# Chunk loop of a Mamba-2 mixer: the order of GpSimd's two additions, the place of ScalarE's scaling, and a second buffer for B and C

## The reference

```
def ssd_chunked(x, dt, a_neg, bm, cm):
    ...
    acs = jnp.cumsum((dt * a_neg)..., axis=2)
    seg = acs[:, :, :, None] - acs[:, :, None, :]
    decay_in = jnp.exp(jnp.where(tri, seg, NEG_INF))
    cb = jnp.einsum('bctgn,bcsgn->bctsg', cc, bc)
    y_diag = jnp.einsum('bctsg,bctsgh,bcsghp->bctghp', cb, decay_in, xdt)
    states = jnp.einsum('bcsgn,bcsgh,bcsghp->bcghpn', bc, decay_out, xdt)
    ... # prev: the state ahead of each chunk, from a scan over chunks
    y_off = jnp.einsum('bctgn,bcghpn,bctgh->bctghp', cc, prev, jnp.exp(acs))
    return y_diag + y_off

y = y_fwd + y_bwd + d_skip * xs
y = y * silu(z)            # then an RMS norm per group of 256 columns
```

## Time and profile before

| | us |
|---|---|
| median of 3 executions | 2486.51 |
| lowest and highest | 2482.69, 2488.45 |
| the profiled execution, its time | 2485.22 |
| the profiled execution, its span | 2483.40 |

### The profile page before, as it was taken

The page is one execution under the profiler, slowest core; times in us unless marked ns, Lnnn a source line. Parts: engine busy times, 40 slices in busy tenths (PEclk is TensorE's granted clock), DMA queues, the critical chain, the costliest instruction groups (busy, mean ns, idle before and its releaser), DMA issues.

```text
span 2483.4 us, 33046 instructions
## 1 busy us (share of the span) xinstructions
PE 2426.9 (98%) x12882; PEld 2072.2 (83%) x12882; DVE 1375.8 (55%) x1561; ACT 998.4 (40%) x1737; POOL 1263.1 (51%) x814
## 2 busy tenths in 40 slices
PE   7999999999999999999999999998999999999999
PEld 6989997887888888887898899977878888888887
DVE  4476557738655546428345765586385555544332
ACT  4345567613444344212024465585144344431110
POOL 3242113323977877666633311142349877866664
PEclk9999999999999999999999999999999999999999
DMA  4434444231222212654333334442212222226544
GB/s 160 136 114 125 134 139 149 81 119 68 85 79 91 85 68 85 217 178 132 130 121 94 110 128 151 134 136 90 89 64 102 85 70 100 83 90 201 174 141 142
DMA packets 102964, 290.68 MB, mean 117 GB/s; under 512 B 7800, under 2 KB 30328, under 8 KB 101112
## 3 DMA queue, kind: packets, MB, share of 16 engines
q1 hardware_dynamic: 80360, 255.73, 30.4%
q10 hardware_dynamic: 22456, 32.90, 4.1%
HBM read 229.84 MB, written 58.75 MB: 116 GB/s over the span
## 4 chain that ended last, share of the span: by engine, by line
PE 81%; DVE 9%; ACT 4%; POOL 3%; issue 2%; DMA 1%; SPq 0%; ACTq 0%; DVEq 0%; POOLq 0%
PE PS L690 20%; PE PS L694 20%; PE PS L693 20%; PE PS L775 3%; PE PS L779 3%; PE PS L778 3%; PE PS L945 2%; PE PS L934 2%; POOL WL L629 2%; DVE HL L1780 1%; PE PS L1116 1%; PE PS L1081 1%; PE PS L924 1%; PE PS L923 1%; ACT LG L1501 1%
## 5 line engine op out<-in xcount | busy, mean ns | idle before, releaser
L605 POOL CAST WH<-RAW 128x1024 fp32r<-128x1024 f32 x156 | 184.5, 1182 | 905.5 <-PE PS L690 327.1
L690 PE MATMUL PS<-HH,WH 128*128 128x512 f32 x1264 | 496.4, 393 | 3.6 <-ACT QS L1668 2.6
L694 PE MATMUL PS<-HH,WL 128*128 128x512 f32 x1264 | 493.3, 390 | 0.0
L693 PE MATMUL PS<-HL,WH 128*128 128x512 f32 x1104 | 430.5, 390 | 0.0
L607 POOL TENSOR_TENSOR WL<-RAW,WH 128x1024 fp32r<-128x1024 f32 x156 | 396.8, 2543 | 12.5
L690 PEld LDWEIGHTS PS<-HH,WH 128*128 128x128 f32 x1264 | 237.4, 188 | 56.5 <-DVE HL L1780 3.5
L694 PEld LDWEIGHTS PS<-HH,WL 128*128 128x128 f32 x1264 | 237.3, 188 | 51.9
L690 PE MATMUL PS<-AR,WH 128*128 128x512 f32 x704 | 276.0, 392 | 2.3 <-DVE X L2208 1.8
L694 PE MATMUL PS<-AR,WL 128*128 128x512 f32 x704 | 275.9, 392 | 0.0
L693 PE MATMUL PS<-AR,WH 128*128 128x512 f32 x704 | 275.2, 391 | 0.0
L775 PE MATMUL PS<-WH,HH 128*128 128x256 f32 (+1 forms) x896 | 261.0, 291 | 1.7 <-ACT KN L1307 1.3
(11 more groups left out here) (274 smaller groups left out, 4677.3 us busy)
## 6 DMA issues: line engine op xcount, KB each, us to landing
RAW<-wst SPq DMA_DIRECT2D x156, 512.0 KB, 3.5
TOE<-toe_d SPq DMA_DIRECT2D x64, 512.0 KB, 3.7
act_d<-CVV SPq DMA_DIRECT2D x22, 1024.0 KB, 4.0
ARL<-act_d SPq DMA_DIRECT2D x88, 256.0 KB, 3.3
RAW<-wst SPq DMA_DIRECT2D x20, 1024.0 KB, 4.9
RAWB<-wst SPq DMA_DIRECT2D x20, 1024.0 KB, 4.9
XBS<-xbc_d SPq DMA_DIRECT2D x24, 512.0 KB, 4.2
xbc_d<-CV ACTq DMA_DIRECT2D x16, 512.0 KB, 3.6
```

Of the source, the lines that this page charges most:

```text
L605: nc.gpsimd.tensor_copy(hi, raw).then_inc(hi_done, 1)
L690: ins = nc.tensor.matmul(out, wh, xh, start=first, stop=False, skip_group_check=onto)
L693: nc.tensor.matmul(out, wh, xl, start=False, stop=False, skip_group_check=onto)
L694: return nc.tensor.matmul(out, wl, xh, start=False, stop=last, skip_group_check=onto)
```

## The change

It has three parts.

1. POOL adds the forward part (`Y1`) to `Y3` first, and the backward part (`Y2`) after it. In `scan` the two blocks change places, and with them the waits for `y12_done` and `y2_ready`.
2. ACT scales the backward part into `Y2` between the first and the second pair of exponentials, after v, and no longer after the second pair.
3. `BC` becomes two buffers, one for even and one for odd chunks. ACT's copy into it waits for the masks and the state of two chunks ago, no longer for those of the chunk before. The new buffers lie in a stretch that is free during the chunk loop.

```diff
-        BC = work("BC", [P, 2, GROUPS, P])
+        BC = place("BC", [P, 2, 2, GROUPS, P], u_at + 25856)
...
                     step.then(nc.gpsimd.tensor_tensor(by_head(Y3[:]), xs, per_head(par_("d_skip")), ALU.mult))
+                    if c:
+                        pool.wait_ge(y12_done, 1 + l * LINKS + c)
+                        ins = nc.gpsimd.tensor_tensor(Y3[:], Y3[:], Y1[:], ALU.add)
+                        if c < LINKS:
+                            step.then(ins)
                     if c < LINKS:
                         pool.wait_ge(y2_ready, l * LINKS + c + 1)
                         ins = nc.gpsimd.tensor_tensor(Y3[:], Y3[:], Y2[:], ALU.add)
-                        if c:
-                            step.then(ins)
-                    if c:
-                        pool.wait_ge(y12_done, 1 + l * LINKS + c)
-                        ins = nc.gpsimd.tensor_tensor(Y3[:], Y3[:], Y1[:], ALU.add)
                     ins.then_inc(y3_ready, 1)
...
-                            last = nc.tensor.matmul(PS[:, 7, g * 256:(g + 1) * 256], BC[:, 0, g, :],
+                            last = nc.tensor.matmul(PS[:, 7, g * 256:(g + 1) * 256], BC[:, par, 0, g, :],
...
-                    act.wait_ge(w_masked, 2 + n * 2)
-                    if c:
-                        act.wait_ge(sf_full, l * LINKS + c)
-                    A(BC[:].rearrange("p a g n -> p (a g n)"), bank(1), ACT.Copy).then_inc(bst_ready, 1)
+                    if n:
+                        act.wait_ge(w_masked, n * 2)
+                    if c >= 2:
+                        act.wait_ge(sf_full, l * LINKS + c - 1)
+                    A(BC[:, par].rearrange("p a g n -> p (a g n)"), bank(1), ACT.Copy).then_inc(bst_ready, 1)
...
                         if j == 1:
                             v_scaled(c)
-                    if c < LINKS:
-                        act.wait_ge(yo_full, n + 1)
-                        act.wait_ge(chunk_done, 1 + n)
-                        for h in range(HEADS):
-                            cols = slice(h * HD, (h + 1) * HD)
-                            last = A(Y2[:, cols], PS[:, 6, cols], ACT.Copy, scale=EACS[:, c, 8 + h:9 + h])
-                        last.then_inc(y2_ready, 1)
+                        if j == 1 and c < LINKS:
+                                act.wait_ge(yo_full, n + 1)
+                                act.wait_ge(chunk_done, 1 + n)
+                                for h in range(HEADS):
+                                    cols = slice(h * HD, (h + 1) * HD)
+                                    last = A(Y2[:, cols], PS[:, 6, cols], ACT.Copy, scale=EACS[:, c, 8 + h:9 + h])
+                                last.then_inc(y2_ready, 1)
...
-                                TT(SEG[par][:, 2 * g], SEG[par][:, 2 * g], BC[:, 1, g, :].unsqueeze(1).to_broadcast((P, 4, P)),
+                                TT(SEG[par][:, 2 * g], SEG[par][:, 2 * g], BC[:, par, 1, g, :].unsqueeze(1).to_broadcast((P, 4, P)),
```

## The result

The changed kernel takes 2502.53 us (median of 6 executions, 2501.4 to 2504.99) against 2484.97 for the kernel before in the same comparison (6 executions, 2482.69 to 2488.45): ratio 1.0071, 95% interval 1.0058 to 1.0084. It is 17.6 us slower. The forecast was slower by 12, 2498, with a range to 2502: the sign and the mechanism came as forecast, the size did not, and the time lies 0.5 us above the range. In the two traces chunks 0 to 6 of the two loops hold 17.0 us of the difference; outside them the traces differ by +1.6 (ahead of the first loop), +1.4 (between the loops) and -1.7 us (behind), which is not explained here.

A forecast was written before the change was run, and what follows sets the result against it. PE was taken as nearly the bound, with a few stalls. Chunks 1 to 6 add 4.89 and 5.74 us, chunks 0 add 1.0: 11.6 us, profiled 2485.2 to 2496.8, median 1.3 higher, 2498 us; range 2489 to 2502.

The forecast's parts named there:

- What bounds a chunk: Chunk loops: PE nearly the bound, with stalls where DVE's mask L2144 is late; chunks of 8.35 and 9.25 us alternate.
- rule A: DVE operations with two SBUF inputs and POOL's exclude each other, first starter first; DVE ends 0.55 after POOL, POOL begins 0.54 after DVE's start.
- The collision that costs: POOL's L655 of the next chunk starts 0.18 before group 1's mask, delaying PE: 9.73 us a chunk, chunks 1 to 5.
- The second BC buffer at nothing: On ACT, it removes a 6.8 us wait in 7 places, but the new wait for `yo_full` swallows it: cost nothing.
- Chunk 0, +0.5 a layer: First chunk of each layer: masks end later, by +0.1 to +1.1 us; 0.5 taken in each layer.
- The sum: Both chunk loops: 4.89 and 5.74 for chunks 1 to 6, plus 1.0 for chunks 0, makes 11.6 us slower.
- Behind the loop PE runs on without DVE or POOL in between: After the chunk loop: the loss is carried to the end whole.
- The wording of the lock in the Trainium skill: DVE holds the lock for its whole instruction: +0.35 a chunk more, some 3.5 us over 10 chunks, 2501.5 us.
- R1: Half the collision: L655 starts after group 1's mask has begun; every chunk 9.01 us, 2491 us in all; chance 0.12.
- R3: Faster: POOL's second add falls into DVE's free time, nothing stalls; chunks 8.35 us, 2481.4 us in all; chance 0.10.
- R2: Slower still: POOL's second add gets ahead of group 0's first mask; 10.1 us a chunk, 2502 us; chance 0.08.
- R4: No change: the gain of the early `y3_ready` and the new collision offset each other, within 5 us; chance 0.04.

The follow-up runs named there:

- experiment 4: The changed kernel with only L655 on POOL waiting for both masks of the chunk before; 2487.55 us, ratio 1.0011 to the kernel before.
- experiment 5: The changed kernel with L655 waiting for the previous chunk's masks and POOL's add of Y2 for its own chunk's masks; 2480.08 us, ratio 0.9978 to before.
- experiment 3: Kernel before with only the second BC buffer and its later waits, 2485.15 us; changed kernel without that part, 2500.28 us.
- The second trace: The changed kernel run once more, unaltered, in a single execution for another trace; 2502.12 us, no ratio.
- experiment 8: The kernel of experiment 5, with the last chunk's add of Y1 on POOL also waiting for both masks; 2478.32 us, ratio 0.9970 to before.
- experiment 6: The changed kernel with PE repeating group 0 products in its stall, chunks 0 to 5: 8 products 2503.42 us, 4 products 2494.97 us.
- experiment 1: The kernel before with only POOL's order changed, Y1 added first and Y2 after it; 2480.62 us, ratio 0.9981 to before.

## Why the prediction was right and where it was wrong

- *What bounds a chunk, and rule A.* Right. The offsets of chunk 2 above stand within 0.07 us of the forecast ones (only PE's idle time there is 0.89, where about 1.1 was forecast), and experiments 4 and 5 take the two collisions away one after the other with the chunk lengths that the rule gives, 9.00 and 8.35.
- *"The collision that costs", 9.73 us a chunk.* Right, 9.73 in most of the chunks; and chunk 6 at 9.01 was 9.00.
- *The second BC buffer at nothing.* Right (experiment 3).
- *Chunk 0, +0.5 a layer, bounds +0.1 and +1.1.* Slightly low. At full clock it is 9.25 to 9.28 against 8.66 and 8.56, +0.6 and +0.7. L655 comes between the masks there as well: with L655 held back (experiment 4) chunk 0 is 8.55.
- *The sum.* This is the step that failed. "Chunks 1 to 5: 5 x 9.73 = 48.65" takes every chunk at full clock; that longer stalls could change PE's clock was put at nothing, without a reason, in the sum and in every rival. The runs show 5.1 us there. Of the 17.0 us by which the two loops grew (70.29+68.62 against 61.43+60.47), 11.6 were forecast; slow chunks hold 1.20+0.16+1.53+1.68=4.6 beyond 9.73, chunk 0 of the first layer 0.5, in a stretch at half clock as well, and chunk 0's own under-sizing the last 0.3. The second trace repeats the total, and filling the stall takes 4.9 out of it (67.00+67.02, 12.1 more than before, where 11.6 were forecast). So the forecast was in effect one for a kernel whose clock holds. The whole time of that filled kernel is 8.8 us above before (7 to 14 by the interval), so the times bear the 12.1 out only roughly.
- *"Behind the loop PE runs on without DVE or POOL in between".* Not so: PE waits for ACT and DVE there too (experiment 8). For the loss in chunks 0 to 6, which delays all engines, it made no visible difference.
- *Why the clock falls* is shown in so far as PE's stalls bring it about: filling them keeps it full, in one trace each of experiment 6's two kernels. Within chunks 0 to 6 it fell in the changed kernel (three times in each of two traces), in the change without the third part (twice), and in ACT's order alone, and in no other kernel; stalls that made chunks of 9.00 (experiment 4) did not bring it down in the one trace. At which chunk it falls differs between executions; what decides that, and how much stall it takes, stays open. The trace of before had a warning that I did not read. In its last chunk, where PE waits 1.43 us for a mask (L2144), the window (columns as in the earlier trace rows) has the clock at 0.77:

```profile
465.99:475.80 9.81, 8.17 (x44) 7.37 (x44) 9.18 (x16) 6.46 (x22) 3.21 (x3) 0.77 0.01 2
```

In the last chunk or right behind it the clock falls in the first layer of every trace but that of the change without the third part, those with filled stalls too, which are filled in chunks 0 to 5 only.

- *The wording of the lock in the Trainium skill* (SBUF — State Buffer, section Who interferes with whom) would have given 2501.5, closer to the measured total, but by 10.08 us a chunk where 9.73 was measured: the total is near for another reason. (The prediction's own lines give a little less: the second add would end at 5.01+1.27=6.28, not at 6.37, and the chunk would take 10.03.) POOL began 0.54 to 0.55 after DVE's start here too (L2144 at 431.16, the add of Y2 at 431.34 with 1.64 in place of 1.27, so from 431.71).
- *The rivals.* R1 (half the collision) did not happen, but experiment 4 is R1 made on purpose; R1 was priced at 2491 and experiment 4 measured 2487.55; its chunks 1 to 6 sum to 108.0, as priced (108.1), but its chunks 0 stay at 8.55 each, where R1 had 0.5 added. R3 (8.35 throughout, 2481.4) did not happen by itself either; experiment 5 makes it with a wait, at 2480.1. R2, priced at 2502, is nearest to the time by luck: it needs POOL's second add ahead of L2144 of group 0, and that add stands behind it (4.49 against 4.31). R4 fell.
- *The range.* It ended with R2 at 2502, and was too narrow on the slow side because every case in it kept PE's clock full.

## What to carry to other kernels

Before moving an operation of POOL, or what it waits for, lay the starts of POOL and of DVE's operations with two SBUF inputs side by side: with the order decided by less than 0.2 us one way or the other, a mask of 0.69 us takes 1.65. The remedy here was a wait, not a new order: POOL's slack is spent behind the masks on purpose, and 17.6 us slower becomes 6 to 8 us faster. POOL's new order alone, without ACT's and without any wait, does nearly as much (2480.62, 5 us faster). And a stall that is added to each round of a loop on PE has to be priced twice, once as the stall and once as what a clock at half does to the chunk in which it falls (1.2 to 1.7 us for each of the three in the first trace).

## What the runs showed of the hardware

- With 0.9 us of useless products in each stall the changed kernel ran in 2494.97 us in place of 2502.53; in its trace PE stayed at 2.4 GHz through chunks 0 to 6, which accounts for 4.9 of it.
- A stretch at half clock that covered L1081 lengthened the chunk by all that L1081 ended later (1.54 and 1.53 us in chunk 5), though PE has 0.89 us of stall further on in the same chunk: that stall waits for masks which themselves wait for L1081.
- On the lock, who starts first wins, down to differences that a profile barely shows. DVE won with its start 0.05 ahead of POOL's (436.57 against 436.62 in experiment 1, and POOL's operation then took 1.78 in place of 1.27), and even with 0.01 ahead, in chunk 0 of the changed kernel, where POOL's L655 took 1.57 in place of 1.04:

```profile
412.32 0.69 DVE L2144 TENSOR_TENSOR SEG<-SEG 128x512 f32<-128x512 f32 x1
412.33 1.57 POOL L655 TENSOR_TENSOR XW<-XS,WST 128x512 f32<-128x512 f32 x1 [1.21 <-ACT XS L1601]
```

POOL won with its start 0.16 ahead of DVE's (434.00 against 434.16 in the changed kernel), with 0.14, and with 0.13 (1634.19 against 1634.32 in experiment 1). Between DVE ahead by 0.01 and POOL ahead by 0.13 the loops of the traces have no pair.
